# Six PSUM banks for the first part of an even layer, and weights rounded one unit at a time in a first layer

## The reference

```python
p = h @ w_in                                  # first layer: 8 RWKV heads = 4 pairs
r, k, v, gate, wd, ad = split_cols(p + mu * (prev - p), RWKV_SIZES)
y = rwkv7_scan(r, decay, k, v, kk, a)         # in chunks of 128 here
...
aq, ak, av, cq, ckv, kr = jnp.split(h @ w_in, cuts, axis=-1)     # even layer
p = probs(q1b, k1) - lam * probs(q2b, k2)     # difference heads
q = _heads(_rms(cq, g_cq) @ w_uq, MLA_HEADS)  # latent heads
kv = _heads(_rms(ckv, g_ckv) @ w_ukv, MLA_HEADS)
p = softmax((q_nope @ k_nope + q_rope @ k_rope) * MLA_SCALE, masked)
...
```

## Time and profile before

| | before |
|---|---|
| median of three runs | 2029.67 us (2027.68 to 2030.76) |
| the profiled execution | 2024.92 us, span 2023.7 us |
| mean granted TensorE clock | 0.992 |
| TensorE busy | 1954.3 us, 97% |
| VectorE busy | 1139.4 us, 56% |
| ScalarE busy | 827.7 us, 41% |
| GpSimd busy | 134.4 us, 7% |
| TensorE's longest waits | 8.9 us (start), 7.4 us (pair 1's triangle) |

### The profile page before, as it was taken

The page is one execution under the profiler, slowest core; times in us unless marked ns, Lnnn a source line. Parts: engine busy times, 40 slices in busy tenths (PEclk is TensorE's granted clock), DMA queues, the critical chain, the costliest instruction groups (busy, mean ns, idle before and its releaser), DMA issues.

```text
span 2023.7 us, 29081 instructions
## 1 busy us (share of the span) xinstructions
PE 1954.3 (97%) x11718; PEld 1574.4 (78%) x11718; DVE 1139.4 (56%) x1853; ACT 827.7 (41%) x1483; POOL 134.4 (7%) x197
## 2 busy tenths in 40 slices
PE   8999998999899999999999999999999999999998
PEld 6766676878676789888888887777779888888886
DVE  7676687765664564454434355666775454344444
ACT  6345542453535444442323243444454444233232
POOL 1100012000000110000000000233220000000000
PEclk9999999999999999999999999999999999999999
DMA  6311020042120233223233232211134223222321
GB/s 236 105 32 33 32 73 11 4 157 97 42 84 11 84 115 105 73 94 104 93 96 101 92 100 83 70 57 63 63 106 134 73 85 103 94 96 93 103 94 63
DMA packets 55251, 169.66 MB, mean 84 GB/s; under 512 B 5904, under 2 KB 11600, under 8 KB 55120
## 3 DMA queue, kind: packets, MB, share of 16 engines
q1 hardware_dynamic: 55120, 167.82, 25.1%
HBM read 165.70 MB, written 2.10 MB: 83 GB/s over the span
## 4 chain that ended last, share of the span: by engine, by line
PE 66%; DVE 2%; ACT 1%; issue 0%; POOL 0%; DVEq 0%; ACTq 0%; POOLq 0%
PE ps L153 64%; PE ps L158 2%; DVE lo L243 0%; DVE lo L1658 0%; DVE wr L172 0%; ACT wr L166 0%; DVE X L1690 0%; ACT hi L1652 0%; DVE X L1754 0%; DVE mla_pr L426 0%; ACT x_pt L469 0%; POOL X L2341 0%; DVE ps L406 0%; DVE mv L303 0%; ACT Y L2218 0%
## 5 line engine op out<-in xcount | busy, mean ns | idle before, releaser
L153 PE MATMUL ps<-hi,wr 128*128 128x512 f32 (+1 forms) x4632 | 1396.6, 381 | 15.2 <-DVE wr L172 8.9
L153 PEld LDWEIGHTS ps<-hi,wr 128*128 128x128 f32 x4632 | 854.7, 188 | 187.7 <-issue 12.8
L153 PE MATMUL ps<-lo,wr 128*128 128x512 f32 (+1 forms) x2316 | 874.3, 378 | 0.0
L153 PEld LDWEIGHTS ps<-lo,wr 128*128 128x128 f32 x2316 | 436.5, 188 | 82.0 <-issue 3.6
L166 ACT ACTIVATE wr<-raw 128x1024 fp32r<-128x1024 f32 x293 | 309.9, 1059 | 327.8 <-PE ps L153 325.6
L172 DVE TENSOR_TENSOR wr<-raw,wr 128x1024 fp32r<-128x1024 f32 x293 | 362.8, 1240 | 141.3 <-ACT wr L166 141.0
L1740 DVE TENSOR_TENSOR X<-X,ps 128x512 f32<-128x512 f32 x72 | 49.5, 688 | 165.4 <-PE ps L153 165.4
L2420 ACT ACTIVATE mlp<-mlp 128x512 f32<-128x512 f32 x64 | 40.4, 632 | 207.6 <-DVE mlp L2400 207.6
L2400 DVE SCALAR_TENSOR_TENSOR mlp<-ps,R 128x512 f32<-128x512 f32 x64 | 44.3, 692 | 90.0 <-PE ps L153 82.8
L2403 DVE TENSOR_TENSOR lo<-mlp,hi 128x512 fp32r<-128x512 f32 x64 | 44.3, 693 | 87.5 <-ACT hi L2424 87.5
L238 ACT ACTIVATE hi<-X,pv 128x512 fp32r<-128x512 f32 x48 | 34.2, 722 | 100.0 <-DVE X L1740 77.5
(11 more groups left out here) (727 smaller groups left out, 1954.2 us busy)
## 6 DMA issues: line engine op xcount, KB each, us to landing
raw<-d_w SPq DMA_DIRECT2D x128, 512.0 KB, 3.4
raw<-d_wkv SPq DMA_DIRECT2D x32, 512.0 KB, 3.5
raw<-d_w_in SPq DMA_DIRECT2D x30, 512.0 KB, 3.5
raw<-d_sb_w_in SPq DMA_DIRECT2D x24, 512.0 KB, 3.4
raw<-d_ev_w_in SPq DMA_DIRECT2D x16, 512.0 KB, 3.5
raw<-d_wq SPq DMA_DIRECT2D x16, 512.0 KB, 3.5
raw<-d_wo SPq DMA_DIRECT2D x16, 512.0 KB, 3.5
X<-d_xT SPq DMA_DIRECT2D x16, 256.0 KB, 5.8
```

What stands on the lines that cost most here:

```text
L153: return pe.matmul(out, lhsT, rhs, start=start, stop=stop, skip_group_check=True)
```

## The change

In the first layer, `weights_ahead` is called in the step "pr" for pairs 0 and 1 only; pairs 2 and 3 make one unit in each step, on DVE and on ACT. In the even layer the ring is banks 0 to 5 until `mla_tensor` ends; then `widen` sets it to banks 0 to 4, in the same step and just before latent head 0 takes bank 5. No arithmetic changes.

```diff
@@ rwkv_vector
-    weights_ahead(K, M, v, weight_lo, 2)
+    if i < 2:
+        weights_ahead(K, M, v, weight_lo, 2)
     weight_lo(K, M, v)
@@ rwkv_scalar
-    weights_ahead(K, M, a, weight_hi, 2)
+    if i < 2:
+        weights_ahead(K, M, a, weight_hi, 2)
     weight_hi(K, M, a)
@@ even_layer
-def even_layer(M, mla, head, diff, front, norms=(), split=()):
+def even_layer(M, mla, head, diff, front, norms=(), split=(), then=()):
     A, B, C = M.even.lanes
-    weave(*norms, chain(mla(), head(0, A), head(1, A)), chain(diff(0, B), diff(2, B), head(2, B)),
+    weave(*norms, chain(mla(), then, head(0, A), head(1, A)), chain(diff(0, B), diff(2, B), head(2, B)),
@@ tensor_program
-    K.ring(*range(5))
+    K.ring(*range(6))
...
-               front_tensor(K, M, pe, ("r1",), "ev_w_out", ("y", 1), M.hi[1], M.lo[1]))
+               front_tensor(K, M, pe, ("r1",), "ev_w_out", ("y", 1), M.hi[1], M.lo[1]), then=widen(K, *range(5)))
```

## The result

The changed kernel took 2039.19 us (median of 11 executions, 2026.42 to 2044.14) against 2029.67 for the kernel before, executed 11 times beside it (2025.16 to 2038.28). The ratio is 1.0045, with a 95% interval of 1.0031 to 1.0060: slower by 0.45%, where 2027.3 us was forecast and 2031.0 was the upper end of the range. Ten of its 11 executions took over 2036 us, one took 2026.42.

A forecast was written before the change was run, and what follows sets the result against it. TensorE, busy for 97% of the span, was taken to bound the kernel, so only its idle and slow stretches could be won. Terms -2.6 - 1.3 - 0.5 + 2.0 = -2.4 us on 2029.67 gave 2027.3 us, range 2023.8 to 2031.0.

The forecast's parts named there:

- The bounding and the waits: Whole kernel: TensorE, busy 97%, bounds it; ra_T's wait near 3.8 us, new waits of 0.9, about 3 and 2.0.
- Difference heads: Even layer, sixth bank: 1.3 us gained in the first heads (bounds 1.2 and 4.0), 0.5 in the second (0.3 and 1.3).
- Hand-over: Start of latent heads: first score waits for bank 0, 2.0 us lost, bounds 1.5 and 2.1.
- rival (1): Hand-over: its 2.0 us idle makes the clock fall, 3.4 us lost; +1.0 in all, 2030.7 us; chance 0.20.
- The forecast without the fall: Whole kernel, clock not falling at the hand-over: -2.4 us, 2027.3 us; chance 0.50.
- First layer: Pairs 2 and 3: ra_T comes 2.65 us earlier; -0.3 and +0.25 make 2.6 us gained, bounds 0.9 and 4.8.
- nearly as much: First layer: DVE lost some 2.8 us beside GpSimd and would still lose nearly that, so ra_T comes 2.4 to 2.9 earlier.
- at most 1.75: First layer: length in us set for DVE's subtraction behind ra_T, giving a new wait of 0.3 before rb_v's use.
- The clock's term: First layer, 317.04 to 320.8 at half rate: 1.9 us lost before, of which 0.25 is taken back.
- The range and the chances: Whole kernel: 2023.8 to 2031.0 us; faster 0.28, slower 0.05, within 0.67.
- sum of two rivals: Hand-over clock fall plus ra_T no earlier: +3.6 us, with run spread 2033.5 to 2034; chance 0.04.
- The schedule part of the forecast: Whole kernel: first layer -2.6, heads -1.3 and -0.5, hand-over +2.0, together -2.4 us.

The follow-up runs named there:

- e3: Kernel before plus six banks, old weights, second ring begun at bank 1, so no hand-over wait; median 2029.01 us, ratio 0.9985.
- e4: Changed kernel with only the second ring's order altered to 1, 2, 3, 4, 0, so no hand-over wait; median 2024.94 us, ratio 0.9982.
- e2: Changed kernel with the weights as before, leaving six banks and the hand-over wait; median 2034.29 us, ratio 1.0020.
- e6: e4 with the moved subtractions behind the evacuations of v of pairs 2 and 3; median 2028.39 us, ratio 0.9982.
- e9: Changed kernel, hand-over wait kept, with the moved subtractions behind the evacuations of v; median 2032.89 us, ratio 1.0015.
- e12: e6 executed once more, unchanged; median 2029.99 us, ratio 0.9997 to before.
- e1: Changed kernel with five banks again, leaving only the moved weights; median 2030.39 us, ratio 0.9999.
- e7: Changed kernel with eight unused 128x512 products put ahead of the first latent score, filling the hand-over wait; median 2032.54 us, ratio 1.0010.
- e8: The changed kernel executed again, with a second trace; median 2040.23 us, ratio 1.0036 to before.
- e10: Kernel before plus the moved weights and the hand-over wait, on five banks; median 2037.49 us, ratio 1.0038.
- e11: e4 executed once more, unchanged; median 2025.75 us, ratio 0.9976 to before.
- e14: Changed kernel with eight extra products some 20 us before the latent heads, shifting the hand-over by 1.8 us; median 2036.98 us.
- e16: e4, without hand-over wait, with eight extra products some 20 us before the latent heads, a shift of 1.8 us; median 2026.05 us.
- e13: Changed kernel with four extra products some 20 us before the latent heads, shifting the hand-over by 0.9 us; median 2039.37 us.
- e15: Changed kernel with eleven extra products some 20 us before the latent heads, shifting the hand-over by 2.5 us; median 2040.02 us.
- e5: Kernel before with its ring of five restarted at bank 1 for the latent heads, adding only the hand-over wait; median 2031.06 us, ratio 1.0001.
- v first: Variant with the moved subtractions behind the evacuations of v, against e4 (e6, e12) or the changed kernel (e9); medians 2028.39, 2029.99 and 2032.89 us.

## Why the prediction was wrong

**The bounding and the waits** were read rightly. Each wait came out within half a microsecond of its forecast, but for ra_T's (4.5 where 3.8 was forecast).

**Difference heads: right.** -1.4 for heads 0 and 1 (forecast -1.3) and -0.5 for heads 2 and 3 (-0.5); the traces of e3 and e4 have -1.3, -1.4 and twice -0.4. For heads 0 and 1 every trace with six banks has -1.2 to -1.5; for heads 2 and 3 those in which the clock fell there (near 600 us: e2, e6, e9, e12) lost 0.9 to 1.1 instead. The wait of 2.9 before the first query product and 2.2 in three waits on db_pr are the ones named.

**Hand-over: the wait right, its price wrong.** 1.96 us against 2.0. The step that failed is the price of rival (1). It took the fall of before at 638, with its own length of 6.9 us at half rate and 3.4 lost, and concluded 2030.7. Behind the hand-over the clock stayed low for 30.7 us in after, and for 17.1 to 30.7 in the eight traces. In before the clock came back in latent scores of 512 columns, a microsecond ahead of the next weight products:

```profile
643.88 1.70 PE L153 MATMUL ps<-mla_kr,mla_qr 64*128 64x512 f32 x2
...
646.31 0.47 PE L153 MATMUL ps<-hi,wr 128*128 128x512 f32 x1
```

In after it came back in such scores too, but those of 128, 256 and 384 columns and the first of 512 had all run at half rate before them:

```profile
657.74 1.16 PE L153 MATMUL ps<-mla_kr,mla_qr 64*128 64x512 f32 x2
```

Why the low stretch is so much longer here no run shows; the place of the fall among the scores is the one difference seen. Between the first score and the lag at 650 the trace loses 8.7 us beyond the wait, net of the 3.2 that before loses to its own fall at 638 and of the 2.1 us wait on mla_pr that half rate hides (5.0 us in four waits became 2.9 in three). The chance was wrong as well. The prediction's own list has a fall behind 7.39, 2.67 and 2.08 us of idle, the last of them among the latent heads, and none behind 1.24; a wait of 2.0 lies by the 2.08, and yet the 1.24 was taken against the rival, which got 0.20. It should have been far higher: 20 of 23 executions took 2034 us or more. The forecast without the fall is the other group, to which the execution of 2026.42 belongs.

**First layer: the term failed, in sign.** Forecast 2.6 us gained; measured 1.0 lost by 345 us in the trace of after, and 1.0 to 1.8 in eight more with the same first layer (e1, e4, e7, e8, e10, e11, e14, e16); the other two, e13 and e15, gained 0.5. (With the old weights e2, e3 and e5 lie 0.1, 0.7 and 0.5 behind before.) ra_T was 2.24 us earlier in after, 2.65 forecast and 2.4 the lower bound, so the contention cost more than the text had put at "nearly as much". Then, in VectorE's timeline of after, answering to the earlier trace rows:

```profile
316.12 1.07 DVE L847 TENSOR_TENSOR ra_T<-ra_T,lm 128x512 f32<-128x512 f32 x1
317.11 2.29 DVE L172 TENSOR_TENSOR wr<-raw,wr 128x1024 fp32r<-128x1024 f32 x1
...
320.99 1.09 DVE L670 SCALAR_TENSOR_TENSOR rb_v<-rb_rt,pv,rb_v 128x511 f32<-128x511 f32 x1
322.00 1.74 DVE L172 TENSOR_TENSOR wr<-raw,wr 128x1024 fp32r<-128x1024 f32 x1
```

and in TensorE's, answering to the earlier trace rows:

```profile
317.34 1.09 PE L158 MATMUL ps<-cst,ra_T 128*128 128x128 f32 x4 [4.49 <-DVE ra_T L847]
...
322.18 2.05 PE L153 MATMUL ps<-center,rb_v 128*128 128x128 f32 x8 [0.69 <-DVE rb_v L670]
324.02 1.06 PE L158 MATMUL ps<-cst,rb_k 128*128 128x128 f32 x4
324.87 1.06 PE L158 MATMUL ps<-cst,rb_a 128*128 128x128 f32 x4
325.59 0.78 PE L153 MATMUL ps<-hi,wr 128*128 128x512 f32 x1
```

where before had, behind the earlier trace rows:

```profile
321.80 0.60 PE L158 MATMUL ps<-cst,rb_k 128*128 128x128 f32 x4
...
322.59 0.48 PE L153 MATMUL ps<-hi,wr 128*128 128x512 f32 x1
```

The subtraction behind ra_T took 2.29 us where "at most 1.75" was set, so the wait on rb_v is 0.69 and not 0.3. The text had looked at GpSimd's work for pair 2 alone; that for pair 3 begins where the moved subtraction now lies:

```profile
315.38 1.27 POOL L1285 TENSOR_TENSOR rc_k<-rc_k,rc_sg 128x512 f32<-128x512 f32 x1 [1.48 <-DVE rc_tmp L1154]
316.60 1.72 POOL L1286 TENSOR_TENSOR rc_a<-rc_a,rc_sg 128x512 f32<-128x512 f32 x1
318.28 1.71 POOL L1290 TENSOR_TENSOR rc_kr<-rc_kk,rc_Sx 128x256 f32<-128x256 f32 x1
```

The Trainium skill (SBUF — State Buffer, "Who interferes with whom") says that a VectorE instruction with two SBUF inputs contends with a GpSimd one that reads SBUF; the 2.29 us against 1.2 alone agree with it.

In after, the slow stretch did not end 3.8 us after the first product on ra_T, as in before, but 9.4 us after it, at 326.7: the products of center and rb_v took 2.05 us instead of 1.05, those behind them 1.06 instead of 0.60. From ra_T's first product to the first one of the gate g (hi,wr) TensorE needed 8.25 us instead of 5.55, 2.7 more, and 0.55 more in the g products at half rate. 2.7 + 0.55 - 2.24 = +1.0. The clock's term, taken at a gain of 0.25, was a loss of some 2.5, and no bound reached there: the lower one (0.9) left the clock out. v first is the test: in e6 no wait, half rate over at 320.3, and the stage gains 2.3 us (its lag went from 1.34 to -0.97); in e9 and e12 it gains 1.1 and 0.9. But the wait on rb_v alone does not decide it. In e13 it is longer, and half rate ended all the same 3.5 us after the first product on ra_T:

```profile
322.72 1.13 PE L153 MATMUL ps<-center,rb_v 128*128 128x128 f32 x8 [0.98 <-DVE rb_v L670]
```

What else has a part in it stays open.

**The range and the chances** failed by treating the clock's fall as one rival with one price. Slower by over 0.2% had 0.05, for the sum of two rivals. The schedule part of the forecast, -2.4, is -0.7 by span times clock (about 2006.3 against 2007.0), part of it lost in the first layer. That e4 and e11, which have no hand-over wait, come out 4.7 and 5.0 us under before, near the forecast's -2.6 - 1.3 - 0.5 = -4.4, is luck: their traces lose 1.0 us in the first layer, and only 1.6 of the gain is in span times clock.

## What to carry to other kernels

An edit that trades one TensorE wait for another is not judged by their sum: a new idle of 2 us at the hand-over cost 1.7 to 13 us in the mean, by what else was changed, and where it was dear most of that was clock. Where a row of the kernel before shows a fall behind an idle of that length, count on it. Before restarting a ring of PSUM banks, count which bank the last take lies in and begin with one that is long free; here the order 1, 2, 3, 4, 0 instead of 0 to 4 turned a loss of 0.45% into a gain of 0.18 and 0.24% (ratios 0.9982 and 0.9976, both intervals under 1). And where the times of a kernel fall into groups, compare the shares of the groups and the mean clock as well as the medians, since an edit far away can move executions from one group to the other.

## What the runs showed of the hardware

- TensorE's clock can stay at half rate for 17 to 31 us although the profile has TensorE busy all the time (30.7 us in after). The same products ran at 1.00 in before, where it was at 1.00 as they began. In all eight traces it came back while latent scores of 384 or 512 columns ran.
- A wait of 1.96 us is enough for a fall, and not always: eight traces with a fall, three without, and those three agree in the moment of the wait to within 0.1 us where they can be compared (22.18 and 22.16 us behind the last fall).
- A shift of 0.9 us, made by adding work, turned 5 long executions of 12 into 7 of 7.
- A 128x1024 subtraction of VectorE took 1.2 us alone, 2.29 with GpSimd's products for pair 3 beside all of it, and 1.74 with the last of them beside its first 0.7 us; two of them had taken 3.45 together, beside those for pair 2 but for the first 0.2 us. A price beside GpSimd taken from one place did not hold at the next.
